# A two-layer decoder kernel: the first stage in sixteen steps, and two narrow panels computed with the weights held still

## What is computed

```python
for i in range(2):
    mem_kv = mem @ mem_w_kv[i]                       # 256 x 2048 @ 2048 x 1024: keys and values
    if i == 0:
        h = x @ mla_w_in[0]                          # columns: c_q 512, c_kv 512, k_r 64, q_mem 512
        # k_r (64 columns) is rotated by positions and serves as rotary key of all heads
    else:
        h = x @ gdn_w_in[0]                          # q, k, v, z, then a_in 12 and b_in 12 columns, q_mem 512
        # a_in, b_in are the gates: decay and beta of every token and head
    ...
```

## Time and profile before

| | us |
|---|---|
| median of 3 runs (2547.47 to 2549.73) | 2547.99 |
| the profiled execution | 2553.81 |
| its span, first to last instruction | 2552.0 |

### The profile page before, as it was taken

One profiled execution on the slowest core, in us unless ns is written; L12 is line 12 of the kernel. 1 busy time (PEld: TensorE's weight loads), 2 busy tenths in 40 slices (PEclk: granted clock), 3 DMA queues, 4 the chain that ended last, 5 costly groups with the idle time before them and its releaser, 6 DMA issues.

```text
span 2552.0 us, 35658 instructions
## 1 busy us (share of the span) xinstructions
PE 2430.4 (95%) x13657; PEld 2118.3 (83%) x13657; DVE 1473.7 (58%) x1538; ACT 1057.3 (41%) x1243; POOL 269.6 (11%) x246
## 2 busy tenths in 40 slices
PE   7999989999999999989999899889899999999997
PEld 6798778888888888879889798878788888888885
DVE  5544558555546555566746647545665565554555
ACT  3445434434434444343523324334444443443443
POOL 4230001001001001010021121210010010000000
PEclk9989999999999999998999999989999999999998
DMA  5654365666666565653523324225465656566654
GB/s 200 182 140 124 102 228 156 191 193 179 197 192 190 195 187 179 211 166 116 166 67 100 124 67 141 83 66 199 139 190 191 190 183 197 180 197 193 187 190 159
DMA packets 234083, 417.16 MB, mean 163 GB/s; under 512 B 23729, under 2 KB 42442, under 8 KB 232394
## 3 DMA queue, kind: packets, MB, share of 16 engines
q1 hardware_dynamic: 232176, 410.57, 51.6%
q10 hardware_dynamic: 1754, 4.35, 0.5%
HBM read 412.77 MB, written 2.10 MB: 163 GB/s over the span
## 4 chain that ended last, share of the span: by engine, by line
PE 53%; issue 33%; DVE 8%; POOL 2%; ACT 2%; ACTq 0%; DMA 0%; POOLq 0%; DVEq 0%
PE quad L535 9%; PE quad L561 8%; PE quad L563 8%; PE quad L562 8%; PE quad L537 5%; PE quad L508 3%; PE quad L510 3%; PE quad L512 3%; DVE wlo L1308 2%; DVE cv L1652 2%; POOL hl L1940 1%; PE quad L854 1%; PE quad L867 1%; ACT whi L953 1%; PE quad L864 1%
## 5 line engine op out<-in xcount | busy, mean ns | idle before, releaser
L1308 DVE TENSOR_TENSOR wlo<-raw,whi 128x1024 fp32r<-128x1024 f32 x760 | 986.2, 1307 | 778.8 <-ACT whi L953 776.2
L953 ACT ACTIVATE whi<-raw 128x1024 fp32r<-128x1024 f32 x760 | 798.6, 1058 | 1023.3 <-PE quad L563 563.8
L535 PE MATMUL quad<-xs,whi 128*128 128x512 f32 x2048 | 727.9, 400 | 8.3 <-DVE xs L1549 3.7
L537 PE MATMUL quad<-xs,wlo 128*128 128x256 f32 x2048 | 576.1, 281 | 0.0
L561 PE MATMUL quad<-whi,hh 128*128 128x512 f32 x1344 | 529.0, 394 | 11.6 <-DVE wlo L1308 6.4
L563 PE MATMUL quad<-whi,hl 128*128 128x512 f32 x1344 | 524.6, 390 | 0.0
L562 PE MATMUL quad<-wlo,hh 128*128 128x512 f32 x1344 | 524.5, 390 | 0.0
L535 PEld LDWEIGHTS quad<-xs,whi 128*128 128x128 f32 x2048 | 386.9, 189 | 106.1 <-DVE wlo L1308 6.9
L537 PEld LDWEIGHTS quad<-xs,wlo 128*128 128x128 f32 x2048 | 388.8, 190 | 0.1
L561 PEld LDWEIGHTS quad<-whi,hh 128*128 128x128 f32 x1344 | 253.5, 189 | 67.6 <-issue 7.2
L563 PEld LDWEIGHTS quad<-whi,hl 128*128 128x128 f32 x1344 | 253.2, 188 | 53.3
(11 more groups left out here) (272 smaller groups left out, 2085.9 us busy)
## 6 DMA issues: line engine op xcount, KB each, us to landing
raw<-in_mlp_w SPq DMA_DIRECT2D x512, 512.0 KB
raw<-in_gdn_w_in SPq DMA_DIRECT2D x105, 512.0 KB
raw<-in_w_out SPq DMA_DIRECT2D x64, 512.0 KB
raw<-in_mem_w_kv SPq DMA_DIRECT2D x32, 512.0 KB
raw<-in_mla_w_in SPq DMA_DIRECT2D x25, 512.0 KB
raw<-in_mla_w_ukv SPq DMA_DIRECT2D x24, 256.0 KB
gb<-in_ln_g SPq DMA_DIRECT2D x4, 1024.0 KB, 6.4
gb<-in_ln_b SPq DMA_DIRECT2D x4, 1024.0 KB, 8.4
```

What stands on the lines that cost most here:

```text
L535: nc.tensor.matmul(both, b.whi[:, slot, k, cols], b.xs[:, :, kt, :], start=start, stop=False, skip_group_check=True)
L537: last = nc.tensor.matmul(ps[:, j, S:2 * S], b.wlo[:, slot, k, cols], b.xh[:, kt, :], start=False, stop=stop, skip_group_check=True)
L953: nc.scalar.activation(b.whi[:, c % NSPLIT], b.raw[:, slot], ACT.Copy).then_inc(sem.hi_ready, 1)
L1308: nc.vector.tensor_tensor(b.wlo[:, c % NSPLIT], b.raw[:, c % NRAW], b.whi[:, c % NSPLIT].bitcast(F32), ALU.subtract).then_inc(sem.lo_ready, 1)
```

## The change

- `mem` is loaded in four DMAs of 512 KB, each with its own semaphore. The twelve small loads go from ACT's queue to SP's, behind the first four weight chunks. ACT makes a one-column copy before anything else, so that its table is loaded then.
- The first stage has 16 steps. PE makes the first turn, and then in step k turn k+1 (the eight of `mem`, then the eight of `x`) and chunk k (the eight of `memk0`, then the eight of `memv0`). The low part of each turn is made by DVE (`turn_low`), no longer by POOL; DVE's step is the copy of turn k+1, the low part of turn k, the split of chunk k+1.
- The vector transposes come after the last step. The sine and cosine work on DVE comes after them, with splits between its parts.
- POOL builds the masks after the rotation of the queries.
- `kr` and `ab` go through the new `panel_short`: two 64-column weight blocks side by side are held still, 256 tokens move, 48 matmuls. The result has features on partitions, in two halves (even and odd row blocks), and is copied to SBUF (`kcol`, `abcol`). After the first chunk of `qm0` or `q0`, `short_rows` turns it back and adds the halves with four matmuls against the identity.
- PE does four chunks of `q0`, not two, before it picks up the gates, and ACT and DVE feed three chunks inside the gate chain.

```diff
+            def panel_short(p, c, ready):
+                slot = c % NSPLIT
+                pe.wait_ge(sem.panel_free, p - 1)
+                pe.wait_ge(sem.lo_ready, c + 1)
+                ready(0)
+                for k in range(KT):
+                    half = k % 2
+                    ps = panel_ps[p % 2][:, 0, half * S:(half + 1) * S]
+                    both = slice((k - half) * ROPE, (k - half + 2) * ROPE)
+                    hi, lo = (w[:, slot].rearrange("p t n -> p (t n)")[:, both] for w in (b.whi, b.wlo))
+                    nc.tensor.matmul(ps, hi, b.xh[:, k, :], start=k == 0, stop=False, skip_group_check=True)
+                    nc.tensor.matmul(ps, hi, b.xl[:, k, :], start=False, stop=False, skip_group_check=True)
+                    last = nc.tensor.matmul(ps, lo, b.xh[:, k, :], start=False, stop=k >= KT - 2, skip_group_check=True)
+                last.then_inc(sem.chunk_used, 1)
...
-            for k in range(8):
-                if k == 4:
-                    pe.wait_ge(sem.mem_in, 16)
-                turn(TURN_AT["mem0"] + k, b.mrow, 2 * k)
-            pe.wait_ge(sem.x_in, 16)
-            for k in range(PANEL):
-                panel_t(PANEL_AT["memk0"], CHUNK_AT["memk0"], PANEL, b.hh, b.hl, after_turn("mem0"), part=(k, k + 1))
-                turn(TURN_AT["x"] + k, b.z, 2 * k)
+            first_turn(0)
+            for k in range(2 * PANEL):
+                if k < 2 * PANEL - 1:
+                    first_turn(k + 1)
+                if k < PANEL:
+                    panel_t(PANEL_AT["memk0"], CHUNK_AT["memk0"], PANEL, b.hh, b.hl, after_turn("mem0"), part=(k, k + 1))
+                else:
+                    panel_r(PANEL_AT["memv0"], CHUNK_AT["memv0"], PANEL, b.hh, b.hl, after_turn("mem0"),
+                            part=(k - PANEL, k - PANEL + 1))
...
-            panel_r(PANEL_AT["kr"], CHUNK_AT["kr"], 1, b.xh, b.xl, after_turn("x", KT), n=ROPE, ck=KT)
-            panel_t(PANEL_AT["qm0"], CHUNK_AT["qm0"], PANEL, b.xh, b.xl, after_turn("x"))
+            panel_short(PANEL_AT["kr"], CHUNK_AT["kr"], after_turn("x", KT))
+            panel_t(PANEL_AT["qm0"], CHUNK_AT["qm0"], PANEL, b.xh, b.xl, after_turn("x"), part=(0, 1))
+            pe.wait_ge(sem.vcol_set, 1)
+            pe.wait_ge(sem.panel_free, PANEL_AT["kr"] + 1)
+            short_rows(b.kcol, sem.kr_t)
+            panel_t(PANEL_AT["qm0"], CHUNK_AT["qm0"], PANEL, b.xh, b.xl, after_turn("x"), part=(1, PANEL))
...
-            turned_panel("q0", 0, 2)
+            turned_panel("q0", 0, 1)
+            pe.wait_ge(sem.panel_free, PANEL_AT["ab"] + 1)
+            short_rows(b.abcol, sem.ab_t)
+            turned_panel("q0", 1, 4)
...
+            feed(1)
+            first_out(0)
+            first_out(1)
+            first_low(0)
+            feed(1)
+            for k in range(1, 2 * PANEL):
+                if k < 2 * PANEL - 1:
+                    first_out(k + 1)
+                first_low(k)
                 feed(1)
```

More of the change, by code:

```diff
@@ L433, in mlp @@
                                    .rearrange("(t p) n -> p t n", p=P))], g * GCH)
-            panel(CHUNK_AT["memk0"], mem_w_kv[0], 0)
+            for ci in range(PANEL):
+                load(CHUNK_AT["memk0"] + ci, whole(mem_w_kv[0], ci * CK, slice(0, CN)))
+                if ci == NRAW - 1:
+                    small_inputs()
             panel(CHUNK_AT["memv0"], mem_w_kv[0], CN)
@@ L567, in panel_r, with short_rows @@
                     last.then_inc(sem.chunk_used, 1)
+            def panel_short(p, c, ready):
[12 more added lines that the diff above has]
+                last.then_inc(sem.chunk_used, 1)
+            def short_rows(src, then):
+                for t in range(TT):
+                    for half in range(2):
+                        eye = b.ident[:, half * ROPE:(half + 1) * ROPE].unsqueeze(1).to_broadcast((P, 2, ROPE))
+                        last = nc.tensor.matmul(pt_ps[:, t * P:(t + 1) * P].rearrange("p (a c) -> p a c", a=2),
+                                                src[:, half, t * P:(t + 1) * P], eye, start=t == 0 and half == 0,
+                                                stop=half == 1, skip_group_check=True)
+                last.then_inc(then, 1)
             def turn(g, src, kts):
@@ L1014, in _, with first_hi @@
-            feed(PANEL)
+            act.wait_ge(sem.const_set, 1)
+            nc.scalar.activation(b.sums[:, 0, 0:1], b.ident[:, 0:1], ACT.Copy)
+            def first_hi(k):
+                if k < 8:
+                    split_turn(TURN_AT["mem0"] + k, b.hh, 2 * k)
+                else:
+                    split_turn(TURN_AT["x"] + k - 8, b.xh, 2 * (k - 8))
+            feed(1)
+            first_hi(0)
+            feed(1)
+            first_hi(1)
+            feed(1)
+            for k in range(2, 2 * PANEL):
+                feed(1)
+                if k == PANEL + NSPLIT - 2:
+                    take_t("memk0", 0, b.km, 0, 1.0)
+                first_hi(k)
@@ L1015, in _ @@
+            feed(3)
             panel_end("memv0")
@@ L1028, in _ @@
             panel_end("kr")
-            for t in range(TT):
-                last = nc.scalar.activation(b.krow[:, t, :], banks("kr")[:, t, 0:ROPE], ACT.Copy)
-            last.then_inc(sem.panel_free, 1)
+            nc.scalar.activation(b.kcol[:, :, :].rearrange("p a s -> p (a s)"), banks("kr")[:, 0, :], ACT.Copy).then_inc(sem.panel_free, 1)
+            act.wait_ge(sem.kr_t, 1)
+            nc.scalar.activation(b.krow[:, :, :, :].rearrange("p t a c -> p (t a c)"), pt_ps[:, 0:S],
+                                 ACT.Copy).then_inc(sem.kr_rows, 1)
             feed(PANEL)
@@ L1167, in _ @@
             panel_end("ab")
[L1168 to L1170 removed]
+            nc.scalar.activation(b.abcol[:, :, :].rearrange("p a s -> p (a s)"), banks("ab")[:, 0, :], ACT.Copy).then_inc(sem.panel_free, 1)
+            act.wait_ge(sem.ab_t, 1)
+            nc.scalar.activation(b.arow[:, :, :], pt_ps[:, 0:S].rearrange("p (t c) -> p t c", t=TT)[:, :, 0:2 * NH],
+                                 ACT.Copy).then_inc(sem.ab_rows, 1)
             act.wait_ge(sem.gate_in, 32)
```

151 lines of the change are left out of this document (83 added, 68 removed).

## The result

The changed kernel takes 2525.04 us (median of four runs, 2520.87 to 2528.69), the kernel before 2548.86 in the same comparison (2547.47 to 2550.61): a ratio of 0.990, 95% interval 0.9888 to 0.9913, or some 24 us. A second comparison with more runs gave 2526.99, ratio 0.9908 (0.9893 to 0.9924). One of the twelve executions of the kernel before in that comparison ran at a granted clock of 0.64 and took 3525 us; the ratio leaves it out, and the median of the other eleven is 2551.10. The forecast was 2532, so half as much again was gained as it said. The direction was right and the size was not. The largest error sits in one place, the second half of the first stage: 11.4 us, more than the whole miss of 7.

The account below looks back on a forecast made before the run. PE bounds the kernel, busy for 95% of 2552.0 us. First stage +6.3, `kr` -10.3 and `ab` -11.8 sum to -15.8 us, taken off the median of 2547.99: 2532 us, range 2524 to 2541.

Parts of the forecast that it names:

- `kr`: Narrow panel before `qm0`: 16.0 us falls to 5.8, following matmuls gain 1.1, `short_rows` costs 1.0; 10.3 us gained.
- `ab`: Narrow panel before `q0`: 16.8 us falls to 5.8, following matmuls gain 1.8, `short_rows` costs 1.0; 11.8 us gained.
- gates: After `ab`: ready 9.7 us after its end, PE asks after 12.6 us of work; cover 2.9 us, no wait.
- The step that failed: First stage: every chunk waits for its turn's low part; steps 5.05 and 4.85 us, `cq` 6.3 us later than before.
- The chain itself: First stage, between two chunks: transposes, DVE's copy, low part and handing to PE, uncovered, 2.1 us a step.
- The first chunk: First stage: runs at the lower clock, 4.8 us, between 4.2 (clock rises early) and 5.1 (not at all).
- The narrow panels: `kr` and `ab`: 48 matmuls of 256 columns at 0.12 us, 5.8 us each, clock stays up, what follows is fast.
- The rival that they would not hold the clock: `kr` and `ab`: matmuls at 0.21 us, 4.4 us more in each, slow start behind; 2544 us, 4%.
- The early start: Start of first stage: data in at 6.9 us, first real matmul at 11.6 us (10.4 to 12.9) against 24.15.
- The rival of a slow clock: First stage: PE waits a third of each step, clock stays at 1.2 GHz, 40 us over fifteen steps; 2572 us, 5%.
- The first rival: First stage: turn hidden after all, steps 3.3 us, stage ends near 64.5 us, kernel 2508 us; 6%.
- What was put at nothing: Sine work, the fifth `ckv` split (up to 1 us if uncovered), POOL's masks and small loads through SP: no cost counted.

Follow-up runs that it names:

- the second execution: The changed kernel run once more, nothing altered, with more rounds: 2526.99 us, ratio 0.9908 to the kernel before.
- the three kernels in which the late chunk leaves a single long wait: Changed kernel with low part first and x's load behind the second split (2517.73 us), low part first only (2521.02 us), low part back on POOL (2523.63 us).

## Why the prediction came out as it did

| step | forecast | measured |
|---|---|---|
| first real matmul | 11.6 us (10.4 to 12.9) | 10.84 |
| end of `memk0` | 51.75 (11.6 + 4.8 + 7 x 5.05) | 51.14 |
| a step with `memk0` | 5.05 | 5.02 |
| a step with `memv0` | 4.85 | 3.20 |
| `memv0` in all | 36.65 | 25.2 |
| vector transposes | 0.5 | 0.47 |
| `cq` starts | 88.9 | 76.82 |
| `kr` | -10.3 | -10.5 (traces), -10.9 (means) |
| `ab` | -11.8 | -12.7 (traces), -11.5 (means) |
| gates | ready 9.7 after ab, cover 2.9 | 7.5, cover 4.9 |

**The step that failed** is the sentence "Chunk k, the next on PE, waits for the low part of turn k", used for all fifteen steps. It holds for the eight chunks of `memk0`. Chunk 8 + j of the stage is chunk j of `memv0`, which multiplies *memory*, turned eight steps earlier, while the turn beside it is one of x. The diff says so: its `panel_r` line has `after_turn("mem0")`. Bubbles of 1.65 us in seven steps are 11.5 us, and that is the difference, 36.65 - 25.2 = 11.4. The run in which `memv0` waits for x put the bubbles back and landed on the forecast, 88.0 against 88.4. With the step mended, the prediction's own numbers give 88.9 - 11.5 = 77.4 for `cq` and 2532 - 11.5 = 2520.5 us; the kernel takes 2525 to 2527. The range reached down to 2524: 2525 lies at its edge, and 0.990 of the earlier median of 2547.99, 2522.5, outside it. A range that took a doubt in this step seriously would have reached to 2520.

That the time came so near the edge is luck. Over the three places that the change touches, the mended forecast has 5.2 + 10.3 + 11.8 = 27.3 us and the traces 28.2; the medians show only some 24. The 3 to 4 us between lie outside these places or in the spread of executions, and their cause stays open. They hid a third of the error in the step.

**The chain itself** was right to 0.03 us (2.07 from the first transpose to the matmul, 18.09 - 16.02, against 2.1), though its parts came from rows in which these operations stood far apart. The first chunk took 5.18 us, just above the upper bound of 5.1: its matmuls went at 0.21 us apart to the end. In the second execution it took 4.77.

**The narrow panels** hold in every point: 5.84 and 5.75 us instead of the 5.8 forecast, 1.05 us for the eight records of `short_rows`, the granted clock at 1.00, and no slow start of what follows. In the median of whole executions they show less, 16.6 us with the panels alone. The rival that they would not hold the clock is out.

**The early start** was forecast at 11.6 and is at 10.84. The load came as expected (6.79 against 6.9) and ACT began at 6.39, since the first chunk was in before the first quarter of `mem`.

**The rival of a slow clock** is out in the changed kernel: three stretches with PE busy for 7.05 of 10 us, and waits of 1.47 us in each step, were granted 1.00. By the Trainium skill (TensorE: Matmul & The Clock Gate, Part 1) activity releases the throttle; in these steps it stayed released. In the three kernels in which the late chunk leaves a single long wait, of 2.38, 3.03 and 3.64 us, the granted clock behind it was 0.50 (1.2 GHz) for some 3 to 7 us, and the chunk took 4.5, 4.3 and 5.3 us instead of 2.95. So each of these waits cost its own length and then 1.4 to 2.3 us by the clock, and those of 1.47 only their length.

**The first rival** (the turn hidden, 64.5 us, 2508) got 6% and half of it happened: in `memv0` the turn was hidden. I gave it a chance for all steps or none, and never asked it of each panel.

**What was put at nothing** and was not: the twelve small loads on SP's queue. "The small loads go through SP while it waits for buffers" is true of SP's instructions and false of the queue: beside x's load they hold weight chunk 4 until 23.7 us. It cost nothing only because the bubbles were there to cover it; once they were gone it was worth 4.3 us (68.8 - 64.5). The rest at nothing held: the masks ran from 179.9 to 203 us beside PE, the fifth `ckv` chunk was split 1.3 us before its time, and the splits in the steps took 1.22 us. With POOL at work one took 2.09. By the Trainium skill (SBUF — State Buffer, SBUF: two separate sides) one of DVE and GpSimd holds a shared pair of ports for a whole instruction, whichever starts first; both durations agree with it, and so does the run with the low part on POOL, where the splits began first and kept their 1.22 us.

## What to carry to other kernels

Before a per-step cost is multiplied by the number of steps, ask of each consumer in turn *which* step's product it reads: in a loop that is made of two panels, the same order of instructions closes a ring in one and not in the other. Of two operations next to each other on an engine, the one that somebody waits for goes first: swapping them was worth 7.5 us at the end of the stage at once, and 12.8 when the late load that the bubbles had covered was mended too. Small loads don't belong in front of a large one on a queue while another queue moves large packets.

## What the runs showed of the hardware that I had not expected

- Two queues on the same DMA engines shared by number of packets, not by bytes: 146 and 146 with 1.20 and 0.05 MB, then 125 and 125 with 1.02 and 0.26 MB; in the changed kernel, in the same 3 us, 151 and 151 with 1.24 and 0.05 MB. With twelve small loads of 0.15 MB in all in front of it and x's 2 MB on the other queue, the split of a weight chunk of 512 KB began 4 us later (23.64 against 19.60).
- The granted clock of 10 to 11 us and of every microsecond up to 16 reads 1.00 in the changed kernel's trace while the matmuls of 256 columns start 0.21 us apart, against the 0.12 of full speed. In the kernel with the low part first, matmuls 0.21 us apart from 26 to 29 us go with a recorded 0.50. At the very start of an execution the spacing of matmuls tells the clock, and the recorded value doesn't.
- Executions differ in stretches where nothing is changed. From the turns in front of the first MLP to mem1 the 17 traces have 716 to 722 us, from those in front of the second to the end 737 to 744; the four of the kernel before alone have 720 to 721 and 738 to 740. Whole times of single executions can't tell edits of 5 us apart; the starts of given instructions in the first 160 us can tell 1.
